# A third place for the first quarter of the pages in the sample attention, and its loops written out

## The reference, cut to what matters

```python
kc_blk, vc_blk = blocks_from_partials(partials, cmp_phi)
imp_s = chunk.reshape(chunk.shape[:3] + (n_sel_blocks, cps)).sum(-1)
_, idx = lax.top_k(score, min(N_SEL, n_sel_blocks))
kv_g = gather_sel(idx)
...
o = gates[:, :, 0, :, :, None] * o_c + gates[:, :, 1, :, :, None] * o_s + gates[:, :, 2, :, :, None] * o_w
```

## Time and profile before

| what | value |
|---|---|
| median of 3 runs | 1157.62 us |
| the profiled execution's own time | 1153.56 us |
| its span, first to last instruction | 1151.9 us |
| TensorE busy | 1020.5 us, 89% of the span |
| VectorE, ScalarE, GpSimd busy | 52%, 26%, 6% |
| mean granted TensorE clock | 0.951 |
| read from HBM | 139.63 MB |
| in the chain that ended last | PE 64%, DVE 13%, DMA 10%, "issue" 5% |

### The profile page before, as it was taken

One profiled execution on the slowest core, in us unless ns is written; L12 is line 12 of the kernel. 1 busy time (PEld: TensorE's weight loads), 2 busy tenths in 40 slices (PEclk: granted clock), 3 DMA queues, 4 the chain that ended last, 5 costly groups with the idle time before them and its releaser, 6 DMA issues.

```text
span 1151.9 us, 17904 instructions
## 1 busy us (share of the span) xinstructions
PE 1020.5 (89%) x6558; PEld 631.3 (55%) x6558; DVE 603.1 (52%) x1341; ACT 297.6 (26%) x721; POOL 72.3 (6%) x124
## 2 busy tenths in 40 slices
PE   4999999999879979899999988768988978888897
PEld 2476676776544444676574474435545556555443
DVE  2105888777436655996000025278885655555213
ACT  4210001010330031111101124255664344333102
POOL 0000000000000000000000023200001111120000
PEclk9999999999889989999999978789999998988999
DMA  7443664453514466763011111420005665565302
GB/s 315 141 115 110 183 182 112 114 167 122 185 38 110 130 253 202 210 191 111 9 65 73 37 56 29 151 73 1 1 1 172 235 244 193 184 217 183 133 1 82
DMA packets 45725, 147.78 MB, mean 128 GB/s; under 512 B 8393, under 2 KB 20170, under 8 KB 38858
## 3 DMA queue, kind: packets, MB, share of 16 engines
q1 hardware_dynamic: 40522, 129.89, 35.3%
q0 software_dynamic: 5120, 16.78, 4.1%
HBM read 139.63 MB, written 15.27 MB: 134 GB/s over the span
## 4 chain that ended last, share of the span: by engine, by line
PE 64%; DVE 13%; DMA 10%; issue 5%; ACT 4%; SPq 4%; POOL 0%; DVEq 0%; ACTq 0%; POOLq 0%
PE PS L1130 58%; PE PS L1133 6%; DMA arena<-in_win 6%; DMA arena<-in_ccmp 2%; DVE arena L2004 2%; DVE arena L1985 2%; SPq L500 2%; SPq L501 2%; ACT arena L1044 1%; DVE arena L1698 1%; DMA arena<-in_cmem 1%; DVE arena L1727 1%; DVE arena L1728 1%; DVE arena L1817 1%; DMA ptab<-in_pages 1%
## 5 line engine op out<-in xcount | busy, mean ns | idle before, releaser
L1130 PE MATMUL PS<-arena 128*32 128x64 f32 (+16 forms) x5460 | 859.5, 382 | 37.5 <-DVE arena L1985 5.2
L1130 PEld LDWEIGHTS PS<-arena 128*128 128x128 f32 (+5 forms) x5460 | 497.8, 153 | 380.7 <-issue 233.1
L1133 PE MATMUL PS<-arena 128*128 128x128 f32 (+3 forms) x1098 | 176.2, 306 | 86.5 <-DMA arena<-in_csel 16.6
L1133 PEld LDWEIGHTS PS<-arena 128*128 128x128 f32 (+3 forms) x1098 | 134.4, 156 | 132.0 <-issue 86.3
L1727 DVE TENSOR_TENSOR arena<-arena 128x2048 f32<-128x2048 f32 x32 | 73.2, 2287 | 15.5 <-DMA arena<-in_ccmp 14.2
L1915 DVE SCALAR_TENSOR_TENSOR arena<-arena 128x576 f32<-128x576 f32 x8 | 5.8, 756 | 129.6 <-ACT arena L963 129.4
L1728 DVE TENSOR_TENSOR arena<-arena 128x2048 f32<-128x2048 f32 x32 | 73.1, 2284 | 0.0
L1044 ACT ACTIVATE arena<-arena 128x512 f32<-128x512 f32 (+3 forms) x96 | 52.7, 551 | 37.2 <-DVE arena L1985 37.0
L501 POOL DMA_DIRECT2D arena<-in_csel x64 | 34.5, 539 | 260.6 <-PE PS L1133 117.8
L1985 DVE CUSTOM_DVE_ANT_0 arena<-PS,arena 128x512 f32<-128x512 f32 (+3 forms) x96 | 41.2, 486 | 6.4 <-PE PS L1130 6.4
L1883 DVE TENSOR_TENSOR arena<-arena,PS 128x512 f32<-128x512 f32 x16 | 11.0, 687 | 63.4 <-PE PS L1130 63.4
(11 more groups left out here) (178 smaller groups left out, 563.2 us busy)
## 6 DMA issues: line engine op xcount, KB each, us to landing
arena<-in_wall SPq DMA_DIRECT2D x20, 2048.0 KB, 9.9
arena<-in_ccmp SPq DMA_DIRECT2D x128, 256.0 KB, 3.8
arena<-in_csel SPq DMA_DIRECT2D x64, 256.0 KB, 5.2
arena<-in_csel POOLq DMA_DIRECT2D x64, 256.0 KB, 5.5
arena<-in_cmem SPq DMA_DIRECT2D x32, 256.0 KB, 4.0
arena<-in_win SPq DMA_DIRECT2D x8, 1024.0 KB, 9.8
out_win_s<-in_win SPq DMA_DIRECT2D x1, 8064.0 KB
arena<-in_xp SPq DMA_DIRECT2D x1, 2048.0 KB, 16.7
```

The source lines that it names most:

```text
L1130: return nc.tensor.matmul(out, lhsT, rhs, start=start, stop=stop, skip_group_check=True)
L1133: return nc.tensor.transpose(out, in_, ident[0:in_.shape[0], 0:in_.shape[0]])
```

## The change

The first quarter gets three places instead of two, used by the turns in rotation (t modulo 3). The third place is made from memory that is no longer needed at that stage: `small` (weights), `CS` (the convolution's states) and `Gate` now share one stretch of 2048 floats, which the place covers. Before it is written for the first time, SP and POOL wait for the store of the convolution's states (`state_out`). The first quarter of turn t + 1 is requested right after the fourth quarter of turn t, and the window of turn t + 1 right after that. For turn 1 the order on SP is: first quarter, window, then the other quarters. The pages' semaphores are regrouped to fit. ScalarE's and VectorE's loop of three trips is replaced by all turns written out. The scratch cells of `stats` move, and the memory behind them starts 2 floats lower.

```diff
-        small = keep(SMALL_W)
-        stats = keep(400)
+        shared = keep(2048)
+        small = shared[:, 0:SMALL_W]
+        CS = shared[:, SMALL_W:SMALL_W + CT * 18]
+        Gate = shared[:, SMALL_W + CT * 18:SMALL_W + CT * 18 + TT * 36].rearrange("p (t c) -> p t c", t=TT)
+        stats = keep(384)
...
-        SKV = [[at(o, 2048).rearrange("p (s c) -> p s c", s=4) for o in quads]
-               for quads in ((8192, 10240, 0, 2048), (4096, 12288, 14336, 16384))]
+        FIRST = [four_pages(a) for a in (at(8192, 2048), at(4096, 2048), shared)]
+        LATER = [[four_pages(at(o, 2048)) for o in quads] for quads in ((10240, 0, 2048), (12288, 14336, 16384))]
+
+        def skv(t, c):
+
+            return LATER[t % 2][c - 1] if c else FIRST[t % 3]
...
         def quad_load(eng, t, c, pages, loaded):
 
-            if t >= 2:
-                eng.wait_ge(sa_used, START.sa_used + 6 * (t - 2) + c + 2)
+            places = 2 if c else 3
+            if t >= places:
+                eng.wait_ge(sa_used, START.sa_used + 6 * (t - places) + c + 2)
             for s in pages:
                 page = eng.value_load(ptab[0:1, NPG * t + 4 * c + s:NPG * t + 4 * c + s + 1], min_val=0, max_val=POOL - 1)
-                eng.dma_start(SKV[t % 2][c][:, s, :], I["csel"][bass.ds(page, 1), :, :].rearrange("a p c -> (a p) c")
-                              ).then_inc(loaded[t % 2][c], 16)
-
-        def sample_phase(eng, front, middle, back, lk=None):
-
-
+                eng.dma_start(skv(t, c)[:, s, :], I["csel"][bass.ds(page, 1), :, :].rearrange("a p c -> (a p) c")
+                              ).then_inc(loaded[c][t % places], 16)
+
+        def sample_phase(front, middle, back):
 
             front(Turn(0, 0, 2), None)
-
-            def trip(i):
-                for n in range(2):
-                    t, nxt = Turn(i, n, 2), Turn(i, n + 1, 2)
-                    middle(t)
-                    front(nxt, t)
-                    back(t, 2)
-
-            if eng is None:
-                for i in range(NB // 2 - 1):
-                    trip(i)
-            else:
-                with eng.Fori(0, NB // 2 - 1) as i:
...
+            for b in range(NB):
+                t = Turn(b // 2, b % 2, 2)
+                middle(t)
+                if b + 1 < NB:
+                    front(Turn(b // 2, b % 2 + 1, 2), t)
+                back(t, 2 if b + 1 < NB else 1)
...
             sp.wait_ge(pa_mix, 6)
+            quad_load(sp, 1, 0, range(2), sa_lo)
+            window(1)
             for t in range(1, NB):
-                for c in range(4):
+                for c in range(1, 4):
                     quad_load(sp, t, c, range(2), sa_lo)
-                window(t)
+                if t + 1 < NB:
+                    if t == 1:
+                        sp.wait_ge(state_out, 16)
+                    quad_load(sp, t + 1, 0, range(2), sa_lo)
+                    window(t + 1)
...
             pool.wait_ge(pa_mix, 6)
+            quad_load(pool, 1, 0, range(2, 4), sa_hi)
             for t in range(1, NB):
-                for c in range(4):
+                for c in range(1, 4):
                     quad_load(pool, t, c, range(2, 4), sa_hi)
+                if t + 1 < NB:
+                    if t == 1:
+                        pool.wait_ge(state_out, 16)
+                    quad_load(pool, t + 1, 0, range(2, 4), sa_hi)
...
                         if j % 2 == 0:
-                            pe.wait_ge(sa_lo[n][j // 2], 32 * (t.i + t.n // 2 + 1))
-                            pe.wait_ge(sa_hi[n][j // 2], 32 * (t.i + t.n // 2 + 1))
+                            places = 2 if j else 3
+                            pe.wait_ge(sa_lo[j // 2][number % places], 32 * (number // places + 1))
+                            pe.wait_ge(sa_hi[j // 2][number % places], 32 * (number // places + 1))
```

More of the change, by code:

```diff
@@ L306, in build, with four_pages @@
         KCp = at(25728, 128).rearrange("p (g n) -> p g n", g=2)
-        SKV = [[at(o, 2048).rearrange("p (s c) -> p s c", s=4) for o in quads]
-               for quads in ((8192, 10240, 0, 2048), (4096, 12288, 14336, 16384))]
+        def four_pages(a):
+            return a.rearrange("p (s c) -> p s c", s=4)
+        FIRST = [four_pages(a) for a in (at(8192, 2048), at(4096, 2048), shared)]
+        LATER = [[four_pages(at(o, 2048)) for o in quads] for quads in ((10240, 0, 2048), (12288, 14336, 16384))]
+        def skv(t, c):
+            return LATER[t % 2][c - 1] if c else FIRST[t % 3]
         SWKT = at(18432, 1024).rearrange("p (g c) -> p g c", g=2)
@@ L393, in build @@
         fut_set = sem("future_set")
-        sa_lo = [[sem(f"sa_pages01_{n}_{c}") for c in range(4)] for n in range(2)]
-        sa_hi = [[sem(f"sa_pages23_{n}_{c}") for c in range(4)] for n in range(2)]
+        sa_lo = [[sem(f"sa_pages01_{c}_{n}") for n in range(2 if c else 3)] for c in range(4)]
+        sa_hi = [[sem(f"sa_pages23_{c}_{n}") for n in range(2 if c else 3)] for c in range(4)]
         (sa_cs, sa_cm, sa_ce, sa_cn, sa_imp, sa_mask, sa_ft, sa_fa, sa_fd, sa_s, sa_m, sa_p,
@@ L413, in build, with step_dve @@
         block = ctx.enter_context(nc.Block())
-        def step_dve(cell=398):
+        def step_dve(cell=382):
             nc.vector.memset(rs(cell, cell + 1), 0.0)
@@ L1078, in took @@
                         if j < 8:
-                            nc.scalar.copy(SKV[t.n % 2][j // 2][:, 2 * (j % 2):2 * (j % 2) + 2, 0:256],
+                            nc.scalar.copy(skv(t.at(1), j // 2)[:, 2 * (j % 2):2 * (j % 2) + 2, 0:256],
                                            PS[:, 6 + j % 2, :].rearrange("p (q c) -> p q c", q=2)).then_inc(sa_fa, 1)
@@ L1116, in back @@
                     nc.scalar.copy(SPT[0], PS[:, 6, :].rearrange("p (s c) -> p s c", s=4)).then_inc(sa_ba, 1)
-            sample_phase(act, front, middle, back)
+            sample_phase(front, middle, back)
             for j in range(TT):
@@ L1579, in front @@
                                 ins = turn(PS[:, 6 + j % 2, 256 * q + 128 * g:256 * q + 128 * g + 128],
-                                           SKV[n][j // 2][:, 2 * (j % 2) + q, 128 * g:128 * g + 128])
+                                           skv(number, j // 2)[:, 2 * (j % 2) + q, 128 * g:128 * g + 128])
                     else:
@@ L1622, in part @@
                 def part(c):
-                    return [(c, 0, 512, lambda p, gp: SKV[t.n % 2][c][p:p + 64, :, 128 * gp:128 * gp + 128])]
+                    return [(c, 0, 512, lambda p, gp: skv(number, c)[p:p + 64, :, 128 * gp:128 * gp + 128])]
                 def new(s):
@@ L1642, in back @@
                 late = tiles[4:]
-                tiles[4:] = [(SM[:, 128 * j:128 * j + 128], SKV[n][j // 4][:, j % 4, 256:512], sel, j == 0, False)
+                tiles[4:] = [(SM[:, 128 * j:128 * j + 128], skv(number, j // 4)[:, j % 4, 256:512], sel, j == 0, False)
                              for j in range(NPG)]
@@ L1672, in _ @@
             pe.wait_ge(pa_mix, 6)
-            sample_phase(None, front, middle, back)
+            sample_phase(front, middle, back)
             pe.wait_ge(sz_done, 1)
@@ L2045, in took @@
                     dve.wait_ge(sa_ft, t.value(10, j + 1, base=START.sa_ft))
[L2046 removed]
+                    tcopy(skv(t.at(1), j // 2)[:, 2 * (j % 2):2 * (j % 2) + 2, 0:256], PS[:, 6 + j % 2, :].rearrange("p (q c) -> p q c", q=2)
                           ).then_inc(sa_fd, 1)
@@ L2095, in masks @@
                         dve.wait_ge(sa_part, t.value(2, 2))
-                        step_dve(396)
+                        step_dve(380)
                     elif c == 0:
                         dve.wait_ge(sa_s, t.value(1, 1, base=START.sa_s))
-                        step_dve(397)
+                        step_dve(381)
                     lk.did(ttr(SM[:, 512 * c:512 * c + 512].rearrange("p (n k) -> p n k", k=SB),
@@ L2148, in _ @@
             lk.link(nc.vector.memset(SSC, 0.0))
-            sample_phase(dve, front, middle, back, lk)
+            sample_phase(front, middle, back)
             dve.wait_ge(sa_done, START.sa_done + NB)
```

15 lines of the change are left out of this document (removed).

## The result

| what | before | after |
|---|---|---|
| median of 3 runs | 1157.62 us | 1141.51 us (1140.48 to 1143.77) |
| the profiled execution's own time | 1153.56 us | 1140.48 us |
| its span | 1151.9 us | 1138.8 us |
| TensorE busy | 1020.5 us | 1018.6 us |
| mean granted TensorE clock | 0.951 | 0.957 |

The ratio of the times is 0.9848, with a 95% interval of 0.9813 to 0.9883. On the medians 16.1 us are won, by the ratio 17.6; the forecast was 21.8 us.

A forecast was written before the change was run, and what follows sets the result against it. TensorE bounds the kernel, idle in the samples' stage for late ends of request bursts. 26.2 - 3.0 - 1.4 = 21.8 us won; 1153.56 - 21.8 = 1131.8, with 4.06 to the median about 1136 us, range 1130 to 1145.

The forecast's parts named there:

- one sign of being wrong: Fronts 2 to 7: fronts still over 11 us and the third quarter late as well would show the forecast wrong.
- The turns of before: Six turns, back(0) to back(6): 147.28 us profiled, 121.1 us without waits for landings, so at most 26.2 us to win.
- The undisturbed turn: Samples' stage: a turn without waits for landings takes 11.83 us plus front(1)'s 8.79 less 0.44, that is 20.18 us.
- The fourth quarter: Fronts 2 to 7: third in its burst, it lands 0 to 0.8 us late; 0.5 taken, 3.0 us in six turns.
- Turn 1: front(1): waits 1.8 us for its fourth quarter instead of 0.44 for the window; 1.4 us lost, bounds 0.44 won, 2.9 lost.
- The clock: TensorE in the fronts: no fall of the granted clock taken; bound 0.9 us in each of six fronts, 5.3 us.
- The loops, the memory, the wait for `state_out`: Loop removal brings nothing, memory moved by 2 floats 0 with 1 us either side, SP's and POOL's new wait holds nothing.
- No wait is for the first quarter: Samples' stage: taking that quarter out of the burst helps because the other three quarters and the window move up.
- a fourth quarter as late as before: Rival, turns' bursts: complete 14.7 us after the first request, 2.9 us late each turn; 1150 us, chance 0.11.
- Code for the written-out loops: Rival, ScalarE and VectorE: code fetches hold a front 6.2 us a turn, six turns lose 37 us; 1173 us, chance 0.06.
- The larger stall at taken branches: Rival, loops: two taken branches stall 6.2 us each, so 12 us more would go; 1124 us, chance 0.04.
- That the change has no effect: Rival, samples' stage: the burst's later start eats what moving up gives, the waits stay; 1157 us, chance 0.07.

The follow-up runs named there:

- the last run: Against the kernel with the third quarter requested a turn ahead: turn 1's third quarter requested while the prompt's attention still runs; 1134.90 us, ratio 0.9797.
- the held run: Against the kernel with the third quarter requested a turn ahead: turn 2's third quarter and window held until front(1) has its window's first half; 1141.76 us, ratio 0.9850.
- run 18: Not a run number: 18 counts the blocks that move in the kernel with turn 2's third quarter and window held back; 1141.76 us, ratio 0.9850.

## Why the prediction was right, and where it was off

The forecast of 1136 us was 5.5 us too low; the measured 1141.51 us is inside its range. The mechanism was right: the waits went where it said, and in the fronts 2 to 7 none took their place but the fourth quarter's. Of its signs, the request 4.0 us behind back, the clock and the window's waits held; four of the six fronts are inside 8.4 to 9.2 us (the others take 10.13 and 9.38), and one sign of being wrong came in front(1), a late third quarter. Its sum was too large by 5.7 us. Step by step:

- **The turns of before.** The 147.28 us were one execution's. Another took 144.65, so 2.6 us of the 26.2 were not there to be won. The offset of 4.06 us, added because the profiled execution lay under the median, did not mend this: where its luck lay (the stretch over the memory), the change has no part. This is the largest single error.
- **The undisturbed turn.** 20.18 us was put together from back(0), middle(1) and front(1). The turns without any wait for a landing take 20.37 us (11.90 + 8.46; five turns of the last run take 20.36 to 20.40). Six turns: 1.1 us.
- **The fourth quarter.** The burst starts 4.02 us behind the first values of back(0), as worked out (918.44 and 914.42 us). Lateness was given as 0 to 0.8 us. The six waits were 0.48, 0.98, 0.78, 0, 2.06 and 1.31 us, 0.94 on the mean where 0.5 was taken, and three of them are above 0.8. The landings that this term went by are those of turn 5, and in the trace of before this was the earliest third quarter of the six turns: TensorE waited 0.67 us for it, and 1.06 to 1.99 us in the other five.

```profile
994.61 1.06 PE L1133 MATMUL PS<-arena 128*128 128x128 f32 x8 [0.67 <-DMA arena<-in_csel]
```

The quarter was in 12.0 us after the burst's first request in turn 5, and 12.4 to 13.4 us in the others, 12.6 on the mean. The fourth quarter of the changed kernel is in after 11.6 to 13.8 us, 12.6 on the mean: the step held, and one turn was too few to price it. The fronts 2 to 7 are longer than 8.46 us by 3.6 us together, because a part of each wait takes the place of a wait for ScalarE's copies. The term was 3.0 us; the run with the third quarter ahead gives it as 2.9.
- **Turn 1.** The loss was given as 1.4 us, with 2.9 as the bound if turn 2's first quarter gets ahead on POOL's queue. It was 1.9 us against the first profile, 2.2 against the second. The step that failed is that only the fourth quarter would be late. The third was late too: needed 2.67 us after the front's start, at 906.4 us, it was in at 907.6. And the next turn's pages did get ahead, as the landing at 907.0 us and the run that holds them back show.
- **The clock.** No fall was taken, and the six turns are at 1.00. That was not certain: behind front(6)'s wait of 2.06 us eight products take 1.06 us, but behind 1.77 us in one experiment they take 1.94, and a second execution of the changed kernel granted 0.85 in front(1).
- **The loops, the memory, the wait for `state_out`.** Zero each. The run in the old order measures loops and memory together at 1.0008; the wait for `state_out` is not in that run, but SP's eight requests across it take 8.37 us, where eight without it took 8.33.
- **No wait is for the first quarter.** This sentence held, and the run with that quarter alone shows how far it reaches: the third place by itself wins nothing. The prediction spoke of the other three quarters and the window moving up together; it did not say that the gain of the pages is owed to the window's leaving. That is the point it missed without harm, since the change did both.

With the four corrections of 2.6, 1.1, 0.6 and 0.8 us the sum of 21.8 becomes 16.7 us, against 16.6 in the profiles and 16.1 on the medians. The corrections are read from the same profiles, so this only says that no term is left over.

The rivals: a fourth quarter as late as before would have made turns of 23.1 us; they take 21.0, and the quarter is in 12.6 us after the first request and not 14.7. Code for the written-out loops would have slowed the run in the old order; it did not, and VectorE's waits named issue from 898 to 1055 us are 0.4 us in the changed kernel. The larger stall at taken branches would have shown there as a gain of 12 us; the interval leaves room for 2. That the change has no effect is what one of its halves does when made alone.

What stays open: why the stretch over the memory takes 39.95 us in one execution and 41.3 to 43.7 in the others. It goes with the granted clock, but no run here changed what sets that.

## What to carry to other kernels

Where a stage waits for a burst of transfers, find the one that lands last and needs to land now, and take that out first; taking out another only hands the wait on, and halves of such an edit may give nothing each by themselves. Give an extra buffer to a piece whose leaving does not make the burst start later, and not simply to the piece that is needed first; here that was worth some 3 us in the profile. Take a landing time from all turns of a trace, not from one. Before a gain is summed against a profile, see from a second execution of the same kernel which stretches vary by themselves.

## What was not expected of the hardware

TensorE stopped for 2.25 and 2.11 us in the middle of a line of products, waiting for no semaphore, in both executions in which turn 2's transfers were held back, and a block on the larger code queue, later than usual, began to move within 0.5 us of the stop's start. Where the block moved ahead of the transfers, TensorE did not stop. The Trainium skill, "Runtime: NRT & Kernel Launch", section "Instruction fetch mechanics", has the cost of going on to the next block mostly hidden. The trace agrees at the other places of this stage: in the held run 18 blocks move from 898 to 1060 us, and TensorE's other waits named issue are 0.9 us in five. Whether this stop is an exception hangs on the reading above, which is not shown. Behind the stop, from 923.32 to 933.10 us, the granted clock averages 0.65, and the 32 products that take 3.65 us otherwise take 5.50 and 5.22: the part with the stop of 2.25 us is 5.6 us longer.

A page took from 2.6 us (the first of turn 2's burst) to 10.9 us (the last of turn 1's) to land, in one kernel. And the halves of an edit on one burst were worth 7 to 9 us and nothing apart, and 16 to 18 together.
